# The feed-forward of a two-layer hybrid encoder step: three parts of 8, 8 and 6 tiles, with the down products of the first two as seven block products for eight

## The reference

```python
uv = jnp.einsum('bld,df->blf', h, w_up)
u, gate = uv[..., :D_FF], uv[..., D_FF:]
u_ext = jnp.concatenate([conv_prev.astype(u.dtype), u], axis=1)
uc = conv_b + sum(conv_w[j] * u_ext[:, j:j + seq] for j in range(CONV_W))
y = jnp.einsum('blf,fd->bld', jax.nn.gelu(uc, approximate=False) * gate, w_down)
```

## Time and profile before

| | |
|---|---|
| median of 3 runs | 1618.62 us (1618.5 to 1618.95) |
| profiled execution, first to last instruction (span) | 1615.2 us |
| outside the span, median less span | 3.4 us |
| PE busy | 1588.6 us, 98% |
| DVE, ACT, POOL busy | 945.3, 648.6, 600.6 us |
| mean granted TensorE clock | 0.998 of full speed |

### The profile page before, as it was taken

The page is one execution under the profiler, slowest core; times in us unless marked ns, Lnnn a source line. Parts: engine busy times, 40 slices in busy tenths (PEclk is TensorE's granted clock), DMA queues, the critical chain, the costliest instruction groups (busy, mean ns, idle before and its releaser), DMA issues.

```text
span 1615.2 us, 40576 instructions
## 1 busy us (share of the span) xinstructions
PE 1588.6 (98%) x18015; PEld 1550.5 (96%) x18015; DVE 945.3 (59%) x1475; ACT 648.6 (40%) x1046; POOL 600.6 (37%) x362
## 2 busy tenths in 40 slices
PE   8999999999999999999999999999999999999998
PEld 7999989899999999999999999898999999999997
DVE  4679556665666216665447894566656650366643
ACT  5555356544333113333254544565433331233322
POOL 5435422223434334344343454122333443334431
PEclk9999999999999999999999999999999999999999
DMA  5222210012233322333322222000223232232331
GB/s 157 66 79 79 66 43 4 4 47 79 79 92 89 90 71 79 87 88 90 91 71 79 73 73 72 11 4 4 73 79 91 79 99 85 66 90 80 94 92 59
DMA packets 218864, 115.41 MB, mean 71 GB/s; under 512 B 9332, under 2 KB 216450, under 8 KB 218690
## 3 DMA queue, kind: packets, MB, share of 16 engines
q1 hardware_dynamic: 218610, 112.79, 24.6%
q10 hardware_dynamic: 80, 0.02, 0.0%
HBM read 109.27 MB, written 3.53 MB: 70 GB/s over the span
## 4 chain that ended last, share of the span: by engine, by line
PE 97%; issue 1%; DVE 1%; DMA 1%; ACT 0%; SPq 0%; DVEq 0%; ACTq 0%
PE ps L658 39%; PE ps L657 39%; PE ps L907 2%; PE ps L910 2%; PE ps L904 2%; PE ps L869 1%; PE ps L881 1%; PE ps L972 1%; PE ps L662 1%; PE ps L1179 1%; PE ps L801 1%; PE ps L676 1%; PE ps L1022 1%; PE ps L964 1%; PE ps L1181 1%
## 5 line engine op out<-in xcount | busy, mean ns | idle before, releaser
L553 POOL TENSOR_TENSOR wlo<-raw,whi 128x1024 fp32r<-128x1024 f32 (+1 forms) x185 | 501.0, 2708 | 750.8 <-ACT whi L1280 750.8
L1280 ACT ACTIVATE whi<-raw 128x1024 fp32r<-128x1024 f32 (+1 forms) x186 | 207.4, 1115 | 622.4 <-PE ps L658 622.4
L657 PE MATMUL ps<-xh,whi 128*128 128x288 f32 x1120 | 331.1, 296 | 1.9 <-DVE xl L1784 1.9
L658 PE MATMUL ps<-xh,whi 128*128 128x288 f32 x1120 | 330.8, 295 | 0.0
L657 PE MATMUL ps<-xl,whi 128*128 128x288 f32 x1120 | 329.9, 295 | 0.0
L658 PE MATMUL ps<-xl,whi 128*128 128x288 f32 x1120 | 328.6, 293 | 0.0
L657 PE MATMUL ps<-xh,wlo 128*128 128x288 f32 x1120 | 328.5, 293 | 0.0
L658 PE MATMUL ps<-xh,wlo 128*128 128x288 f32 x1120 | 328.5, 293 | 0.0
L657 PEld LDWEIGHTS ps<-xh,whi 128*128 128x128 f32 x1120 | 210.2, 188 | 3.9 <-issue 3.2
L657 PEld LDWEIGHTS ps<-xh,wlo 128*128 128x128 f32 x1120 | 210.4, 188 | 0.0
L658 PEld LDWEIGHTS ps<-xh,whi 128*128 128x128 f32 x1120 | 210.2, 188 | 0.2
(11 more groups left out here) (329 smaller groups left out, 3168.3 us busy)
## 6 DMA issues: line engine op xcount, KB each, us to landing
raw<-in_ffn_w_up SPq DMA_DIRECT2D x88, 512.0 KB, 3.8
raw<-in_w_in SPq DMA_DIRECT2D x52, 512.0 KB, 3.7
raw<-in_ffn_w_down SPq DMA_DIRECT2D x32, 704.0 KB, 4.4
raw<-in_w_out SPq DMA_DIRECT2D x16, 512.0 KB, 3.8
xin<-in_x_prompt SPq DMA_DIRECT2D x4, 512.0 KB, 6.4
out<-xin SPq DMA_DIRECT2D x8, 256.0 KB, 2.9
out<-RW SPq DMA_DIRECT2D x16, 64.0 KB, 2.2
g<-in_rwkv_g SPq DMA_DIRECT2D x2, 256.0 KB, 2.9
```

The lines of the kernel that those rows point to most:

```text
L553: e.tensor_tensor(wlo[s][:, 0:width], raw[s][:, 0:width], whi[s][:, 0:width].bitcast(F32), ALU.subtract).then_inc(w_lo[s], 1)
L657: e.matmul(acc(out)[:, 0], lhsT, rhs[:, 0:HT], start=start, stop=stop)
L658: return e.matmul(acc(out)[:, 1], lhsT, rhs[:, HT:TOK], start=start, stop=stop)
L1280: e.activation(whi[s][:, 0:width], raw[s][:, 0:width], ACT.Copy).then_inc(w_hi[s], 1)
```

## The change

The 22 tiles of a layer's feed-forward are cut in three parts, `PARTS` = 8, 8 and 6. The last part is as before, with 6 tiles for 11. In the two others ("folded") a pair of down tiles (outputs 2it and 2it+1) is computed as a 2 by 2 block product: the weights' blocks A11 and A12 are the even and odd feature tiles for the first output tile, A21 and A22 for the second; B11, B12 (even features) and B21, B22 (odd features) are the two halves of the tokens. Seven products do for eight, with sums of blocks as operands: S1 = A21 + A22, S2 = A11 + S1, S4 = A12 + S2 on DVE, S3 = A11 + A21 on GpSimd, each 512 columns wide (`Q`), and T1 to T4 of the activations, 288 columns each, made on DVE while the up tiles run. A product is 4 feature tiles by three passes, 12 matmuls.

Each of the seven weight blocks is rounded by ACT (`quad_hi`) and gets its rest from GpSimd (`quad_rest` for A11, A12, A22, and S3's) or DVE (`quad_lo` for S1, S2, S4). Two partial results are copied from bank to bank by ACT so that later products add to them (b and c of `folded_copies`), one is copied to SBUF (v). DVE adds to x in six pieces of 288 columns (`folded_add`). A pair takes four banks; the next one the other four. In each folded part's second pair two matmuls more open the banks that ACT will write.

In the last up tile of a folded part (`fold`), ACT rounds A11 in place of the next slot 0 tile, and A12, S1, S2, S3, S4 in place of the slot 1 tile and ahead of rounding the activations, A22 behind. DVE makes the sums S1, S2, S4 behind the convolution, and the three rests behind the whole tile. SP holds a pair's loads until S4 of the pair before it has been made.

The core of the diff. Left out are renamings, buffers, semaphores, `quad_rest` (wait, subtract, increment), `quad_hi` (wait for the product that last read the block and for its source, then copy to float32r) and `quad_lo` (wait for `quad_hi`, subtract):

```diff
-FT = F // P // HALVES
+FF = F // P
+PARTS = (8, 8, 6)
+FOLDED = len(PARTS) - 1
+F_AT = (0, 8, 16)
+FH = PARTS[0] // 2
+Q = FH * P
...
+PE_D = ["P1", "P6", "P2", "P7", "P3"]
+AC_D = ["A11", "S1", "S2", "S3", "S4"]
+QUADS = ["A11", "A12", "S1", "S2", "S3", "S4", "A22"]
+AC_C = ["b", "v", "c"]
+SUMS = ["S1", "S2", "S3", "S4"]
+DV_S = ["S1", "S2", "S4"]
+DV_L = ["S1", "S2", "S4"]
+DV_X = ["v12", "v22", "c22", "c12"]
+HT_B11, HT_T1, HT_B21, HT_B22, HT_T2, HT_T3, HT_T4 = range(7)
+SLOT = dict(A12=0, A22=1)
+PRODUCTS = dict(P1=("A11", HT_B11), P5=("S1", HT_T1), P6=("S2", HT_T2), P2=("A12", HT_B21),
+                P7=("S3", HT_T3), P3=("S4", HT_B22), P4=("A22", HT_T4))
...
+                for g, n in enumerate(PARTS):
+                    for it in range(0, n):
+                        if it == 0 and g > 0:
+                            sp.wait_ge(d_sum, nth(DV_S, folded(l, g - 1, KT // 2 - 1), "S4"))
                         for s in range(2):
-                            load(s, turn(s, l, PAIRS["ffn"] + h * FFN_PAIRS + it),
+                            load(s, turn(s, l, ffn(g, it)),
...
+                        if it > 0 and g < FOLDED:
+                            sp.wait_ge(d_sum, nth(DV_S, folded(l, g, it - 1), "S4"))
...
+                        if g < FOLDED:
+                            m = folded(l, g, it)
+                            quad_rest(m, "A11")
+                            po.wait_ge(w_loaded[1], 16 * turn(1, l, ffn(g, n + it)) + 16)
+                            e.tensor_tensor(by_tile(sums[:, 2]), A["A11"], A["A21"], ALU.add).then_inc(p_sum, 1)
+                            quad_rest(m, "A12")
+                            po.wait_ge(d_hi, nth(AC_D, m, "S3"))
+                            e.tensor_tensor(D_lo["S3"], sums[:, 2], D_hi["S3"].bitcast(F32), ALU.subtract).then_inc(p_lo, 1)
+                            quad_rest(m, "A22")
+                        else:
+                            for s in range(2):
+                                split(s, turn(s, l, ffn(g, n + it)), n * P)
...
+                    if quad == "A11":
+                        pe.wait_ge(d_rest, m + 1)
+                    elif quad[0] == "A":
+                        pe.wait_ge(w_lo[SLOT[quad]], own[SLOT[quad]] + 1)
+                    elif quad == "S3":
+                        pe.wait_ge(p_lo, m + 1)
+                    else:
+                        pe.wait_ge(d_lo, nth(DV_L, m, quad))
+                    for j in range(FH):
+                        if it == 0:
+                            pe.wait_ge(f_dve, (t + 2 * j + (1 if col in (HT_B11, HT_T1) else 2)) * len(F_DV))
+                        wh, wl = D_hi[quad][:, j * P:(j + 1) * P], D_lo[quad][:, j * P:(j + 1) * P]
+                        e.matmul(out, wh, Hhi[:, col, j], start=fresh and j == 0, stop=False, skip_group_check=True)
+                        e.matmul(out, wh, Hlo[:, col, j], start=False, stop=False, skip_group_check=True)
+                        mm = e.matmul(out, wl, Hhi[:, col, j], start=False, stop=j == FH - 1, skip_group_check=True)
...
+                def folded_pair(g, it):
+
+                    m = folded(l, g, it)
+                    a, v, b, c = quad_banks(it)
+                    own = [turn(s, l, ffn(g, PARTS[g] + it)) for s in range(2)]
+                    if it == 0:
+                        pe.wait_ge(psum_free[0], own[0])
+                        pe.wait_ge(n_rs, 2 * (l * NORMS + 1) + 2)
+                    if it == 1:
+                        pe.wait_ge(d_rest, m + 1)
+                        for o in (b, c):
+                            e.matmul(o, D_hi["A11"][:, 0:P], Hhi[:, HT_B11, 0], start=True, stop=True, skip_group_check=True)
+                    if it >= 2:
+                        pe.wait_ge(psum_free[0], own[0] - 1)
+                    product(g, it, "P1", a, True)
+                    product(g, it, "P5", v, True)
+                    pe.wait_ge(d_copy, nth(AC_C, m, "b"))
+                    product(g, it, "P6", b, False)
+                    product(g, it, "P2", a, False)
+                    pe.wait_ge(d_copy, nth(AC_C, m, "c"))
+                    product(g, it, "P7", b, False)
+                    product(g, it, "P3", c, False)
+                    pe.wait_ge(d_add, nth(DV_X, m, "c22"))
+                    product(g, it, "P4", b, False)
...
+                    ac.wait_ge(d_prod, nth(PE_D, m, "P1"))
+                    ac.wait_ge(psum_free[1], own if it == 0 else own - 1)
+                    e.activation(b, a, ACT.Copy).then_inc(d_copy, 1)
+                    ac.wait_ge(tile_done[0], turn(0, l, ffn(g, PARTS[g] + it)) + 1)
+                    if m >= 2:
+                        ac.wait_ge(d_add, nth(DV_X, m - 2, "v22"))
+                    e.activation(vs[it % 2][:, :], v, ACT.Copy).then_inc(d_copy, 1)
+                    ac.wait_ge(d_prod, nth(PE_D, m, "P6"))
+                    e.activation(c, b, ACT.Copy).then_inc(d_copy, 1)
...
+                    if fold:
+                        quad_hi(g, 0, "A11")
+                    elif f > 0:
+                        tile(0, k[0], width)
...
+                    if fold:
+                        for name in QUADS[1:6]:
+                            quad_hi(g, 0, name)
+                    else:
+                        tile(1, k[1], width)
                     ac.wait_ge(f_dve, t * len(F_DV) + F_DV.index("h1") + 1)
-                    e.activation(HH(it), hf[:, :], ACT.Copy).then_inc(f_hi, 1)
-
-                def HH(it):
-                    return hh[:, it, :] if isinstance(it, int) else hh[:, bass.ds(it, 1), :].squeeze(1)
-
-                for h in range(HALVES):
-                    last_half = h == HALVES - 1
-                    for it in range(0, FT - 1):
-                        widen_tile(h, it, KT * P)
-                    widen_tile(h, FT - 1, FT * P)
-                    added(l, PAIRS["ffn"] + h * FFN_PAIRS + FT, (l + 1) * NORMS if last_half else None, FT * P,
-                          0 if last_half and l == DEPTH - 1 else KT * P, last_half)
+                    if g == FOLDED:
+                        e.activation(hh[:, it, :], hf[0], ACT.Copy).then_inc(f_hi, 1)
+                    elif it % 2 == 0:
+                        ac.wait_ge(f_mix, (l * F_AT[FOLDED] + f) // 2 * 4 + 1)
+                        e.activation(Hhi[:, 0:2, it // 2, :], h_first[:, 0:3:2, :], ACT.Copy).then_inc(f_hi, 1)
+                    else:
+                        ac.wait_ge(f_mix, (l * F_AT[FOLDED] + f) // 2 * 4 + 4)
+                        e.activation(Hhi[:, 2:7, it // 2, :], h_second[:, :, :], ACT.Copy).then_inc(f_hi, 1)
+                    if fold:
+                        quad_hi(g, 0, "A22")
+
...
+                    for it in range(0, KT // 2):
+                        folded_copies(g, it)
+                        if it + 1 < KT // 2:
+                            for name in QUADS:
+                                quad_hi(g, it + 1, name)
...
+                    if name == "S1":
+                        dv.wait_ge(w_loaded[1], 16 * own[1] + 16)
+                        dv.wait_ge(w_loaded[0], 16 * own[0] + 16)
+                    if m > 0:
+                        dv.wait_ge(d_lo, nth(DV_L, m - 1, name))
+                    out = by_tile(sums[:, SUMS.index(name)])
+                    if name == "S1":
+                        terms = A["A21"], A["A22"]
+                    elif name == "S2":
+                        dv.wait_ge(d_sum, nth(DV_S, m, "S1"))
+                        terms = A["A11"], by_tile(sums[:, 0])
+                    else:
+                        dv.wait_ge(d_sum, nth(DV_S, m, "S2"))
+                        terms = A["A12"], by_tile(sums[:, 1])
+                    e.tensor_tensor(out, *terms, ALU.add).then_inc(d_sum, 1)
...
+                    if name == "v12":
+                        dv.wait_ge(d_copy, nth(AC_C, m, "v"))
+                        e.tensor_tensor(first[:, HT:TOK], first[:, HT:TOK], vs[it % 2][:, :], ALU.add).then_inc(d_add, 1)
+                    elif name == "v22":
+                        e.tensor_tensor(second[:, HT:TOK], second[:, HT:TOK], vs[it % 2][:, :], ALU.subtract).then_inc(d_add, 1)
+                    elif name == "c11":
+                        dv.wait_ge(d_prod, nth(PE_D, m, "P2"))
+                        e.tensor_tensor(first[:, 0:HT], first[:, 0:HT], a, ALU.add).then_inc(psum_free[0], 1)
+                    elif name == "c22":
+                        dv.wait_ge(d_prod, nth(PE_D, m, "P7"))
+                        dv.wait_ge(d_add, nth(DV_X, m, "v22"))
+                        e.tensor_tensor(second[:, HT:TOK], second[:, HT:TOK], b, ALU.subtract).then_inc(d_add, 1)
+                    elif name == "c12":
+                        dv.wait_ge(d_prod, nth(PE_D, m, "P3"))
+                        dv.wait_ge(d_add, nth(DV_X, m, "v12"))
+                        e.tensor_tensor(first[:, HT:TOK], first[:, HT:TOK], c, ALU.add).then_inc(d_add, 1)
+                    else:
```

(78 more changed lines are left out.)

194 lines of the change are left out of this document (143 added, 51 removed).

## The result

The changed kernel takes **1646.65 us** (four runs, 1645.68 to 1647.68) where the kernel before takes 1618.56 on the same chip (1617.72 to 1618.95): the ratio of the times is **1.0174**, 95% interval 1.016 to 1.0189, so it is slower by 28.1 us. The profiled execution took 1647.34 us with a span of 1645.6, 30.4 more than the span before, and its mean granted clock was 0.987 for 0.998.

What follows compares the result with a forecast made beforehand. It took the order of TensorE's matmuls to bound the kernel (PE 97% of the chain). Terms -24.3 + 36.4 + 11 + 6 + 0.5 = +29.6 us on 1618.6 gave 1648, range 1622 to 1668.

Steps and rivals of the forecast that it cites:

- The gain: Down tiles of both layers: 184 matmuls fewer at 132.2 ns each, 24.3 us less.
- The first pair: Each folded part's first pair: TensorE waits 9.1 us for S1's rest, four times, 36.4 us; bounds 22 to 39.
- Turns between DVE and GpSimd: DVE instructions with two SBUF inputs and GpSimd's alternate whole; first wait 9.1 us, or 5.5 if GpSimd never interferes.
- The clock: Behind the four long waits the clock falls to 0.50 for about 3 us, 1.5 us lost each: 6 us, bounds 0 to 12.
- The pairs: Pairs behind the first: P4 waits for c22, then P5 and P6; 0.7 us for each of 16, 11 us, bounds 0 to 24.
- The slower rival: In the pairs, PSUM adds also take turns, or raw[1] comes 2 us late: 29 us more, 1677; chance 0.11.
- Its other half, late loads: Load of raw[1] comes 2 us late in each pair, delaying A22's rest and S1; shares the 1677 case's 0.11.
- The parts and the last part: Last part's first tile waits up to 0.3 us for `hl` in each layer, 0.5 us; the rest fits.
- The 3.4 us that the prediction adds outside the span: Whole kernel: the median lies 3.4 us above the profiled span, 1615.2 against 1618.6.
- The first rival: GpSimd seldom in the way: first waits 5.5 to 7 us, pairs at 11.1, 1620 to 1632; 0.20 for 1622 to 1635.

Runs made afterwards that it cites:

- e7: Changed kernel with all of GpSimd's work for the folded pairs (rests and S3's sum) replaced by zeros: 1627.71 us, 1.0065 of the kernel before.
- e1: Changed kernel with GpSimd's rests of A12, S3 and A22 in each folded part's first pair set to zero: 1635.03 us, 1.0127 of the kernel before.
- e4: Changed kernel with DVE's rests of S1, S2, S4 ahead of scaling the gate and ACT rounding the sums before A12: 1636.28 us, 1.0127.
- e2: Changed kernel with 56 useless matmuls behind P1 in each folded part's first pair, keeping TensorE busy: 1635.73 us, 1.013 of the kernel before.
- e5: Changed kernel with DVE taking c22 between the next pair's sums S1 and S2: 1645.22 us, 1.0173 of the kernel before.
- e3: Changed kernel with nothing folded, only the parts of 8, 8 and 6 tiles: 1616.73 us, 1.0011 of the kernel before.
- e9: Changed kernel with the first pair's order laid out anew, v added from its PSUM bank, c22 between S1 and S2: 1625.71 us, 1.0048 of the kernel before.
- e10: Changed kernel with v added to x from its PSUM bank and c22 between S1 and S2, first pair not relaid: 1645.78 us, 1.0175.

## Why the prediction held, step by step

It gave 1648 and the mechanism is the one that it named; the measured terms are set beside its own.

- **The gain, -24.3 us.** Confirmed: 184 matmuls fewer, at 0.13 us apart (504.40, 504.54).
- **The first pair, +36.4.** Measured 34.2. By the chain's own marks, counted from 491.39: products with the gelu done at 2.7 (laid out: 2.8), mixtures at 4.85 (5.4), the big rounding at 6.3 (6.9), `Hlo` at 8.0 (8.5), S1's rest at 9.7 (10.5). The gate's scaling ended later than laid out (1.1 for 0.8: S4's sum still stood ahead of it), GpSimd's turns sooner: S3's rest at 3.8 for 4.1, A22's at 9.2 for 9.8. Behind them the first mixture took another 0.3 us and S1's rest 0.5, where 0.45 and 0.7 were laid out.
- **Turns between DVE and GpSimd.** e7 takes them away and leaves 5.6 us for the laid out 5.5; e1 takes only the rests of that pair away and leaves 6.1. They are 10 to 12 of the 34 us. The larger part is the dependence itself: the last up tile, its mixtures, two roundings, in a row, with nothing for TensorE to do. e4 shows that moving the sums' rests alone takes only some 10 of the 34 us off.
- **The clock, +6.** Mis-sized: 8.3 in the trace and 8.4 by e2. The row that it came from the earlier trace rows had a half-speed stretch of 3 to 3.5 us; behind these longer idle stretches two of the four ran on for 5.6 and 6.1 us. The Trainium skill (TensorE: Matmul & The Clock Gate, HAM oscillation) says that repeated gaps cost this way, which the rows above agree with.
- **The pairs, +11.** Mis-sized: 6.3. P4 does wait for c22, twelve times and not sixteen (a part's last pair has no sums of a next one ahead of it), 0.41 us from start to start and not 0.7. The waits of P5 and P6 that were put beside it are near nothing in the changed kernel and appear only when c22 goes ahead (e5). The turns are real but come in one burst of a pair, shown in the timelines of DVE and GpSimd:

```profile
508.31 1.75 POOL L730 TENSOR_TENSOR Tall<-raw 128x512 f32<-128x512 f32 x1
509.01 1.60 DVE L2583 TENSOR_TENSOR Tall<-raw,Tall 128x512 f32<-128x512 f32 x1
510.01 1.73 POOL L715 TENSOR_TENSOR wlo<-raw,whi 128x512 fp32r<-128x512 f32 x1
510.53 0.44 DVE L2613 TENSOR_TENSOR x<-x,ps 128x288 f32<-128x288 f32 x1
510.89 1.41 DVE L2583 TENSOR_TENSOR Tall<-raw,Tall 128x512 f32<-128x512 f32 x1
512.22 1.80 DVE L2588 TENSOR_TENSOR wlo<-Tall,whi 128x512 fp32r<-128x512 f32 x1
```

  DVE's 512-wide instructions take 1.4 to 1.8 us for 0.69 and GpSimd's 1.7 for 1.27, but the rest of the pair has room enough for both.
- **The slower rival, refuted.** The addition from PSUM at 510.53 ran wholly beside GpSimd's 510.01 to 511.74 and took 0.44 us. It takes no turn. (The Trainium skill, SBUF — State Buffer, Who interferes with whom, had said so of instructions with at most one SBUF input; this row agrees.) Its other half, late loads, showed in the first pairs only. The page, and a row of the waits:

```profile
raw<-in_ffn_w_down SPq DMA_DIRECT2D x32, 512.0 KB, 3.9
...
POOL Tall L730 <- DMA raw<-in_ffn_w_down: 6.3, 4, 2.4
```

  GpSimd's sum S3 waited for a load once in each part, ahead of P1; in the third part (at 1297.4) DVE's S1 did too, for 0.65 us, and the whole last up tile came late by it: that part's wait is 8.84 for the first one's 8.38. In the pairs that follow no sum waited for a load.

- **The parts and the last part, +0.5.** 1.5 for both layers by e3.
- **What is left.** The terms that were measured sum to -24.3 + 34.2 + 6.3 + 8.3 + 1.5 = 26.0; the span grew by 30.4 and the median by 28.1. For the span the difference lies in the recurrent stage, which the change doesn't touch. Its windows in the two layers, of the kernel before and of the changed one:

```profile
201.23:333.17 131.94, 126.54 (x3938) 117.21 (x3936) 83.45 (x230) 78.78 (x201) 33.12 (x53) 1.00 0.06 16
991.30:1125.57 134.27, 127.16 (x3938) 117.36 (x3936) 83.52 (x230) 78.60 (x201) 33.13 (x53) 1.00 0.07 16
```

```profile
201.30:334.64 133.34, 126.76 (x3938) 117.36 (x3936) 83.66 (x230) 78.89 (x201) 33.20 (x53) 1.00 0.06 16
1005.35:1142.68 137.33, 127.81 (x3938) 117.84 (x3936) 83.73 (x230) 78.85 (x201) 32.97 (x53) 1.00 0.06 16
```

  The same instructions take 266.2 and 270.7 us; in e3 they took 261.1, in e9 265.4, in e10 270.0. TensorE's waits there stand mostly under "issue", 7.3 us before and 10.9 after. The cause stays open. That the median grew by less than the span has a plain reason: executions of the kernel before for which a span is on record take 1.7 to 1.9 us more than it, so the profiled one (span 1615.2) took about 1616.9, under its median, where the changed kernel's profiled one lay 0.7 above its own. The 3.4 us that the prediction adds outside the span is made of both: 1.7 outside it and 1.7 of this difference. Errors thus met: the pairs were put 4.7 us and the first waits 2.2 too high, the clock 2.3 and the parts 1.0 too low, and the rest (2.1 us of the median's growth, 4.5 in the two profiles) comes, by the profiles, from a stage that no step of the prediction spoke of. That the forecast lies 1.4 us from the measured time is luck in part; the path and its largest term it had right. (The first rival's upper end, 1632, doesn't come from its own terms: 1618.6 - 24.3 + 28 + 6 is 1628.)

That folding could pay with a better order stays open as well. e9 has 25.4 us of waits in pieces and 1.5 of clock to set against 24.3. Its folded parts are within 2.6 us of unfolded ones and the cutting into parts costs 1.5 more; the span of its profiled execution is 2.9 us over the kernel before's, its recurrent stage 0.8 shorter. But that execution was the fastest of six, and the median of e9 is 8.7 above the kernel before's: where the others spend the rest no trace shows.

## What to carry to other kernels

When matmuls are saved by making their operands out of other results, lay out the chain from the last such result to the first product that needs it, engine by engine in the order of their queues, and set it against the saving once for every time that the pipeline starts. Here one start cost 8.5 us of waiting and 2 of clock against 6.1 saved by all four pairs behind it. Slack averaged over a stage says nothing of that moment; and when one wait is removed, the next operand in line is only as early as the engine that makes it last.
